# Input projections of a two-layer hybrid backbone: seven block products per pair of tiles in place of eight, weights in five column blocks

## What is computed

```
h_lat = rmsnorm(x, norm_g) * (1.0 + scale[:, None]) + shift[:, None]
h_ctx = rmsnorm(ctx, norm_g) * (1.0 + scale_c) + shift_c
s_lat = split_cols(h_lat @ w_in)
s_ctx = split_cols(h_ctx @ w_in)
...
q = jax.nn.silu(s["hg_q"]); z = s["hg_f"]
logf = jnp.logaddexp(log_lb, log_1mlb + jax.nn.log_sigmoid(z)); kk = (1.0 - lbh) * jax.nn.sigmoid(-z)
xbc = jax.nn.silu(dwconv_centred(s["ss_xbc"], conv_w, conv_b))
y = jnp.concatenate([br[0] for br in branches], axis=-1) @ w_out
```

## Time and profile before

| | us |
|---|---|
| median of three runs (5851.4 to 5854.6) | 5852.31 |
| the profiled execution's own time | 5848.45 |
| its span, first to last instruction | 5846.7 |
| layer 0's projection, first to last product | about 1136 |
| TensorE busy | 5392.3 (92% of the span) |
| VectorE busy | 2994.9 (51%) |
| ScalarE busy | 1701.4 (29%) |
| GpSimd busy | 2398.8 (41%) |
| DMA, mean over the span | 91 GB/s |

### The profile page before, as it was taken

One profiled execution on the slowest core, in us unless ns is written; L12 is line 12 of the kernel. 1 busy time (PEld: TensorE's weight loads), 2 busy tenths in 40 slices (PEclk: granted clock), 3 DMA queues, 4 the chain that ended last, 5 costly groups with the idle time before them and its releaser, 6 DMA issues. The chain is left out here.

```text
span 5846.7 us, 74555 instructions
## 1 busy us (share of the span) xinstructions
PE 5392.3 (92%) x25984; PEld 2843.0 (49%) x25984; DVE 2994.9 (51%) x5002; ACT 1701.4 (29%) x4084; POOL 2398.8 (41%) x1761
## 2 busy tenths in 40 slices
PE   5999999987888799999889999999678889999989
PEld 2445445436777533333445544544467763333334
DVE  1444444444777655551334455455557766555324
ACT  1121121122344244444112212212224432444422
POOL 0112212223444279998211112111234434999941
PEclk7999999986999899999899999999779998999999
DMA  6233233247222100000543333332462211000022
GB/s 241 86 104 101 99 100 102 96 170 238 89 91 95 57 1 8 8 1 6 214 149 109 101 99 103 101 98 95 138 200 97 95 51 46 1 8 8 5 110 106
DMA packets 358609, 530.08 MB, mean 91 GB/s; under 512 B 89344, under 2 KB 233528, under 8 KB 351904
## 3 DMA queue, kind: packets, MB, share of 16 engines
q1 hardware_dynamic: 332818, 457.34, 23.6%
q10 hardware_dynamic: 19728, 40.41, 1.8%
q0 software_dynamic: 5760, 28.36, 1.4%
HBM read 371.61 MB, written 154.08 MB: 90 GB/s over the span
## 5 line engine op out<-in xcount | busy, mean ns | idle before, releaser
L607 PE MATMUL psum<-group_W,projection_hT 128*128 128x512 f32 (+3 forms) x4304 | 1686.1, 547 | 5.9 <-DVE projection_hT L729 5.7
L2277 POOL TENSOR_TENSOR attention_PS<-attention_PS 128x1024 f32<-128x1024 f32 x548 | 1265.7, 2350 | 81.2 <-ACT attention_PS L2410 72.9
L607 PEld LDWEIGHTS psum<-group_W,projection_hT 128*128 128x128 f32 x4304 | 814.2, 190 | 841.6 <-issue 805.8
L2323 DVE TENSOR_REDUCE attention_mxp<-psum 128x1 f32<-128x512 f32 (+1 forms) x1016 | 654.5, 686 | 541.6 <-PE psum L2460 541.6
L459 POOL TENSOR_TENSOR projection_cx<-projection_cx,projection_cw 128x768 f32<-128x768 f32 x102 | 188.4, 1847 | 1684.9 <-DMA projection_cw<-in_ss_conv_w 1684.9
L2410 ACT ACTIVATE attention_PS<-psum 128x512 f32<-128x512 f32 (+1 forms) x1168 | 630.6, 591 | 717.3 <-PE psum L2514 689.4
L2460 PE MATMUL psum<-attention_QK 32*128 32x512 f32 (+1 forms) x2592 | 771.5, 611 | 9.1 <-DVE attention_mxp L2312 6.1
L2508 PE MATMUL psum<-attention_QK 32*128 32x512 f32 x2336 | 664.3, 642 | 0.0
L2526 PE MATMUL psum<-attention_PS,attention_va 128*64 128x512 f32 x2336 | 627.7, 616 | 0.0
L607 PE MATMUL psum<-projection_W,projection_hT 128*128 128x512 f32 (+3 forms) x1424 | 563.0, 538 | 8.3 <-DMA projection_W<-in_w_in 8.3
L680 ACT ACTIVATE projection_ut<-psum 128x256 f32<-128x256 f32 (+2 forms) x322 | 127.5, 407 | 1426.5 <-PE psum L607 1416.4
(11 more groups left out here) (386 smaller groups left out, 6627.1 us busy)
## 6 DMA issues: line engine op xcount, KB each, us to landing
u<-projection_ut SPq DMA_DIRECT2D x240, 256.0 KB, 2.0
projection_cx<-xbc SPq DMA_DIRECT2D x306, 128.0 KB, 2.2
projection_cw<-in_ss_conv_w SPq DMA_DIRECT2D x102, 384.0 KB, 4.5
mixing_hg<-u SPq DMA_DIRECT2D x34, 1024.0 KB, 5.0
group_W<-in_w_in SPq DMA_DIRECT2D x8, 2316.0 KB, 18.9
output_y<-y SPq DMA_DIRECT2D x34, 512.0 KB, 4.1
xbc<-projection_ut SPq DMA_DIRECT2D x34, 384.0 KB, 2.4
projection_cx<-in_ss_conv_b SPq DMA_DIRECT2D x102, 128.0 KB, 3.7
```

The source lines that it names most:

```text
L607: ins = nc.tensor.matmul(ps[n % RING][:, lo - c0:lo - c0 + w], hT[b][:, q], W[q][:, lo:lo + w], start=(q == 0), stop=(q == KT - 1))
L2277: G.tensor_tensor(SA[x % 2][:, rs, 0:w], one[:, rs, 0:w], PT[i % PTB][:, rs, 0:w], ALU.add) \
L2323: bk.release(V.tensor_reduce(mxp[x % 2][:, q:q + nn, 2 * pr + j, a], bk[job, j][:, 0:nn * (hi - lo)].rearrange("p (q n) -> p q n", q=nn), ...
```

## The change

The projection of both layers is written anew; modulation, output and the allocation of weights follow.

- The columns are sorted into five blocks (`COLUMNS`), each with a left and a right half of up to 512 columns (268 in block 3). The tiles go in nine pairs, the pairs in three groups of three. The order is group, block, pair; one pair in one block is called a **quad** here, and 3.1 is block 3, second pair of its group. 45 quads a layer.
- A quad takes seven products of 4 matmuls each (P1, P6, P7, P5, P2, P4, P3) into four banks A, B, D, E. ScalarE copies P1 out of A and P2's sum to `u`; VectorE makes yy = P6 + P1, ff = P7 + yy, C22 = P5 + ff, then P4 + yy and P3 + yy. TensorE waits for p1 ahead of P2, for ff ahead of P4 and for C22 ahead of P3; the next quad's P1 waits for A, its P7 for D and its P5 for E. In the last layer the context pair is multiplied directly ("simple").
- VectorE makes T1 and T2 of the next block in the last quad of a block; GpSimd makes T3 and T4 there, and S1 to S4 once a pair.
- Weights are held for two blocks only (`k.raw`) and loaded again in each of the three groups (57 MB a layer for 19 MB). SP issues the load when a block's first quad starts.
- What follows the product (gates, rotation, forget gate) runs one quad later, in four steps (`stage1` to `stage4`) placed between the additions. Gates are Exp on ScalarE, then +1, reciprocal and product on VectorE, as before, for both tiles at once and from SBUF instead of PSUM.
- The convolution goes in two pieces of 384 columns a tile, assigned to quads by `CONV`: one a quad from quad 1.1 on; the groups have 10, 12 and 14 pieces for 11, 11 and 10 places, so that a second piece comes into 3.0 in group 1 and into 3.0, 3.1, 3.2, 4.0 in group 2 (groups are counted from 0).
- In the output stages GpSimd no longer waits for the weights; SP loads two weight blocks of layer 1 during output0.

```diff
+COLUMNS = [([(OFF["ss_xbc"], 512)], [(OFF["ss_xbc"] + 512, 256), (OFF["ss_z"], 256)]),
+           ([(OFF["hg_f"], 512)], [(OFF["hg_q"], 256), (OFF["hg_i"], 256)]),
+           ([(OFF["da_q"], 512)], [(OFF["ml_o"], 256), (OFF["ml_z"], 256)]),
+           ([(OFF["da_z"], 256), (OFF["ml_i"], 12)], [(OFF["hg_z"], 256), (OFF["ml_i"] + 12, 4), (OFF["ss_dt"], 8)]),
+           ([(OFF["ml_v"], 256), (OFF["da_v"], 256)], [(OFF["ml_q"], 512)])]
 BANKS = 8
...
+def load_block(k, eng, l, i, some):
+
+    for n in some:
+        at = 0
+        for lo, w in COLUMNS[i % len(COLUMNS)][n % 2]:
+            rows = k.x["w_in"][l, (n // 2) * 512:(n // 2 + 1) * 512, lo:lo + w].rearrange("(k p) n -> p k n", p=P)
+            eng.dma_start(k.raw[i % 2][n][:, :, at:at + w], rows).then_inc(k.b_in[i % 2], 16)
+            at += w
...
+    TURN = {0: 1, 1: 2}
+    for g in range(GROUPS - 1):
+        TURN[quad_of[g, NB - 1, 1]] = 3 * g + 3
+        TURN[quad_of[g, NB - 1, 2]] = 3 * g + 4
+        TURN[quad_of[g + 1, 0, 0]] = 3 * g + 5
+    CONV_TILES = [range(0, 5), range(5, 11), range(11, NT)]
+    CONV = {q: [] for q in range(N)}
+    jobs = []
+    for g in range(GROUPS):
+        some = [(g, c, t) for c in range(2) for t in CONV_TILES[g]]
+        slots = [quad_of[g, b, j] for b in range(1, NB) for j in range(MEMBERS)][1:]
+        if g == GROUPS - 1:
+            slots = slots[:-1]
+        extra = [quad_of[g, b, j] for b, j in ((3, 0), (3, 1), (3, 2), (4, 0))][:max(0, len(some) - len(slots))]
+        for job, q in zip(some, sorted(slots + extra)):
+            CONV[q].append(len(jobs))
+            jobs.append(job)
...
+                def taps(m):
+                    g, c, t = jobs[m]
+                    part = slice(c * CWD, c * CWD + CWD)
...
+                    for a in range(3):
+                        sp.dma_start(cx[:, a], k.xbc[t + 1, a:a + P, part]).then_inc(s["taps_in"], 16)
...
+                for q in range(N):
+                    if first_of(q) and 1 <= inst(q) < INST - 1:
+                        sp.wait_ge(s["product"], products(q))
+                        load_block(k, sp, l, inst(q) + 1, range(4))
+                    if CONV[q]:
+                        taps(CONV[q][0])
+                    if q:
+                        store(q - 1)
+                    if len(CONV[q]) > 1:
+                        taps(CONV[q][1])
...
+                for q in range(N):
+                    if q and simple(q - 1):
+                        gp.wait_ge(s["product"], products(q))
+                        t3(inst(q))
+                    for m in CONV[q]:
+                        convolve(m)
+                    if last_of(q) and q + 1 < N:
+                        if not simple(q + 1):
+                            t3(inst(q + 1))
+                        produced(gp, q, "P4")
+                        t4(inst(q + 1))
+                    if q in TURN:
+                        sums(TURN[q])
...
-                def products(r, b, n, kind):
...
-                    for q in some:
-                        ins = nc.tensor.matmul(ps[n % RING][:, lo - c0:lo - c0 + w], hT[b][:, q], W[q][:, lo:lo + w],
-                                               start=(q == 0), stop=(q == KT - 1))
...
+                    at_least(pe, s["free_A"], made("A", q))
+                    product("A", a11, b11, w, True)
+                    at_least(pe, s["free_B"], made("B", q))
+                    pe.wait_ge(s["t12_made"], 2 * i + 2)
+                    pe.wait_ge(s["sums_made"], 4 * p + 2)
+                    product("B", S2, T2, w, True)
+                    at_least(pe, s["free_D"], made("D", q))
+                    pe.wait_ge(s["t3_made"], i + 1)
+                    pe.wait_ge(s["sums_made"], 4 * p + 3)
+                    product("D", S3, b12, w, True)
+                    at_least(pe, s["free_E"], made("E", q))
+                    product("E", S1, T1, w, True)
+                    if q in TURN:
+                        turn(TURN[q])
+                    pe.wait_ge(s["p1_made"], full(q + 1))
+                    product("A", a12, b21, w, False)
+                    pe.wait_ge(s["t4_made"], i + 1)
+                    pe.wait_ge(s["ff_made"], full(q + 1))
+                    product("D", a22, T4, w, False)
+                    pe.wait_ge(s["c22_made"], full(q + 1))
+                    pe.wait_ge(s["sums_made"], 4 * p + 4)
+                    product("E", S4, b22, w, False)
...
+                def conv_gate(m):
+                    act.wait_ge(s["conv_sum"], m + 1)
+                    A(cx[:, 1], cx[:, 0], ACT.Exp, scale=-1.0).then_inc(s["conv_sig"], 1)
...
+                    for m in CONV[q][:1]:
+                        conv_gate(m)
...
+                        produced(act, q, "P2")
+                        A(u[q % 2][:, 0, 0:w], bank["A"][:, 0:w], ACT.Copy).then_inc(s["free_A"], 1)
+                    for m in CONV[q][1:]:
+                        conv_gate(m)
...
+                        z, sig = v[:, :, 768:1024], e[:, :, 256:512]
+                        st.then(V.tensor_scalar(e[:], e[:], 1.0, None, ALU.add))
+                        V.reciprocal(v[:, :, 512:768], e[:, :, 0:256])
+                    else:
+                        z = v[:].rearrange("p t (h n) -> p t h n", h=2)[:, :, :, 0:256]
+                        sig = e[:].rearrange("p t (h n) -> p t h n", h=2)
+                    if b != 2:
+                        st.then(V.tensor_scalar(sig, sig, 1.0, None, ALU.add))
+                    st.then(V.reciprocal(sig, sig))
+                    V.tensor_tensor(z, z, sig, ALU.mult).then_inc(s["gated"], 1)
+
...
+                def stage2(q):
+                    n = of_block(1, q + 1)
+                    if block(q) == 1:
+                        z = u[q % 2][:, :, 0:512]
+                        dve.wait_ge(s["lf_log"], n)
+                        at_least(dve, s["st_kk"], 16 * (n - 1))
+                        if l:
+                            st.then(V.scalar_tensor_tensor(h1[:], z, 0.0, h1[:], ALU.min, ALU.subtract))
+                            st.then(V.tensor_tensor(h1[:], h1[:], lbr[:, 0].unsqueeze(1).to_broadcast([P, 2, 512]), ALU.add))
+                            V.tensor_tensor(h2[:], h1[:], z, ALU.subtract).then_inc(s["lf_key"], 1)
+                        else:
+                            V.scalar_tensor_tensor(h2[:], z, 0.0, h1[:], ALU.max, ALU.add).then_inc(s["lf_key"], 1)
+                            V.scalar_tensor_tensor(z, z, 0.0, h1[:], ALU.min, ALU.subtract).then_inc(s["lf_done"], 1)
+                        return
+                    if block(q) == 2:
+                        rotate(q, 1)
+                    multiply(q)
...
+                def stage3(q):
+                    n = of_block(1, q + 1)
+                    if block(q) == 1 and l:
+                        z = u[q % 2][:, :, 0:512]
+                        lb1 = lbr[:, 1].unsqueeze(1).to_broadcast([P, 2, 512])
+                        dve.wait_ge(s["lf_key"], n)
+                        st.then(V.tensor_tensor(z, h1[:], lb1, ALU.subtract))
+                        V.scalar_tensor_tensor(h0[:], z, -1.0, z, ALU.mult, ALU.min).then_inc(s["lf_neg2"], 1)
+                        st.then(V.tensor_tensor(h1[:], h1[:], lb1, ALU.max))
+                    if block(q) == 1:
+                        multiply(q)
...
+                def convolved(m):
+                    dve.wait_ge(s["conv_sig"], m + 1)
+                    st.then(V.tensor_scalar(cx[:, 1], cx[:, 1], 1.0, None, ALU.add))
+                    st.then(V.reciprocal(cx[:, 1], cx[:, 1]))
+                    at_least(dve, s["st_conv"], 16 * m)
+                    V.tensor_tensor(co[:], cx[:, 0], cx[:, 1], ALU.mult).then_inc(s["conv_done"], 1)
...
+                    if q:
+                        stage1(q - 1)
+                    if not simple(q):
+                        produced(dve, q, "P6")
+                        dve.wait_ge(s["p1_made"], full(q + 1))
+                        V.tensor_tensor(yy[:, 0:w], bank["B"][:, 0:w], p1[:, 0:w], ALU.add).then_inc(s["free_B"], 1)
+                    if q:
+                        stage2(q - 1)
+                    if not simple(q):
+                        produced(dve, q, "P7")
+                        dve.wait_ge(s["free_B"], made("B", q + 1))
+                        V.tensor_tensor(ff[:, 0:w], bank["D"][:, 0:w], yy[:, 0:w], ALU.add).then_inc(s["ff_made"], 1)
+                    if q:
+                        stage3(q - 1)
+                    if not simple(q):
+                        produced(dve, q, "P5")
+                        dve.wait_ge(s["ff_made"], full(q + 1))
+                        at_least(dve, s[f"st_u{q % 2}"], stored(q - 2))
+                        V.tensor_tensor(v[:, 1, 512:512 + w], bank["E"][:, 0:w], ff[:, 0:w], ALU.add).then_inc(s["c22_made"], 1)
+                    if last_of(q) and q + 1 < N:
+                        t12(inst(q) + 1, 1)
+                        t12(inst(q) + 1, 2)
+                    if q in TURN:
```

(16 more changed lines are left out.)

786 lines of the change are left out of this document (384 added, 402 removed).

## The result

The changed kernel takes **5950.54 us** in the median (5943.75 to 5956.28) against 5853.45 (5851.4 to 5857.88) for the kernel before: a ratio of 1.0164, 95% interval 1.0147 to 1.0182. Forecast were 5871 us and a range up to 5940. The sign, slower, had the larger chance; the size was missed: the profiled execution, 5950.89 us, lies 102.4 us above that of before, where the sum gave 19. The result lies in the band of the prediction's "port or further waits" (5900 to 6030), which had a chance of 0.25.

What follows compares the result with a forecast made beforehand. TensorE, busy 92% of the span, was taken to bound the kernel, chiefly by projection matmuls. From 5848 us, 303 saved and 322 given back made 5867; with 3.9 for the median, 5871 us, range 5790 to 5940.

Steps and rivals of the forecast that it cites:

- port or further waits: Outcome band of 5900 to 6030 us, for the shared SBUF port deciding or more waits; chance 0.25.
- What takes time away: Both projections: seven products for eight save 141.5 us in layer 0 and 126 in layer 1, together 267.
- The starts and tails: Projections' beginnings and ends: gains of 9 us at layer 0's start, 3 at layer 1's, 8 for both tails.
- the outputs: Both output stages: GpSimd's sums no longer wait for weights, so the second product starts earlier; 16 us saved.
- the sum of the stalls: Waits added in the projections: 135 us in layer 0 and 187 in layer 1, 322 in all.
- Stalls in front of ff: TensorE's sixth product waits behind VectorE's gates: 1.75 us each in 2.1 and 2.2, 6.2 in 3.1 and 3.2.
- the queue: At block starts, taps land behind weights at about 16 us: 3.0 loses 9.75 us, 2.0 loses 2, per group.
- the rule that I had weighed: SP's DMA queue: each engine consumes descriptors in ring order; had taps overtaken weights, 3.0 would be about 1 us shorter.
- The step that failed: Layer 1's forget gate: VectorE operations meeting GpSimd end after it, 1.86 instead of 0.69 us; whole term 52 us.
- The rival of 6016 us: SBUF port: GpSimd lengthens VectorE's two-tensor operations by 1.17 us, 200 us in all; band 5900 to 6030, chance 0.25.
- Doubled quads: Quads with a second convolution piece, a 14 us chain: 12.5 us lost in group 1, 34 in group 2.
- new convolution weights: Convolution chains of groups 1 and 2: newly loaded weights add 3 us each, within 52 us a layer.

Runs made afterwards that it cites:

- e3: Changed kernel with SP issuing the convolution piece's store and taps and the previous quad's stores ahead of the next block's weight load: 5962.0 us.
- e2: Changed kernel with T3 and T4 of the weights made by VectorE in place of GpSimd: 5929.8 us.
- e4: Changed kernel with the convolution pieces spread over more quads, double places only in 4.0 and 4.1 of group 2: 5845.3 us.
- e7: Changed kernel with ScalarE's copy of P2 (in context quads, their copies) ahead of the convolution piece's Exp: 5948.7 us.
- e1: Changed kernel with the gates' sigmoids on ScalarE (Exp, Ln, Exp) in place of VectorE's +1 and reciprocal: 5852.7 us.
- e8: Kernel before with only the output change: GpSimd makes the first pair's sums ahead of its weight wait and next-layer loads: 5841.2 us.

## Why the prediction missed

**What takes time away** was right. By the undisturbed quads (24.03 and 12.66 us) it is 142.5 us in layer 0, forecast 141.5, and 129 in layer 1, forecast 126. A product step is 0.858 us where I had 0.865, a narrow one 0.452 where I had 0.473. The starts and tails gave 28 us, forecast 20; the outputs 12.6, forecast 16. What failed is the sum of the stalls: 322 us forecast; with the narrow step as measured, 179 us in layer 0 and 234 in layer 1.

**Stalls in front of ff** were sized rightly in the quads computed: 2.2 and the narrow ones with one piece are within 1 us of the forecast lengths, 3.0 in groups 1 and 2 too (in group 0, where it waits for new convolution weights as well, it is 2.4 us longer). In layer 1, where GpSimd's T3 and T4 were counted, 2.0 of groups 1 and 2 lost 13.6 and 13.4 us for 13.2. e3 bears out the queue as well: issued ahead of the weights, the taps of 3.0 landed early and the quad of group 0 took 21.5 us for 25.4. By that the rule that I had weighed (the Trainium skill, DMA: Bandwidth & Descriptors, Queues, rings and completion order) agrees with the runs.

**The step that failed** is the one on GpSimd beside VectorE. I counted it for the forget gate of layer 1 alone and gave the rival a flat 1.17 us on half of all operations. What the trace shows is neither: a few operations are held until a long one of GpSimd ends (0.35 us becomes 4.67), at each turn of a block, and quads behind it pay. In layer 0, 2.0, 2.1 and 4.0 lost 51.5 us where I had 24.3. e2 shows what of the whole gap is T3 and T4: 21 us of run time, net of the 4.6 us a turn that VectorE took on. For 4.0 of group 0 I had written no loss at all and it was 6.5 us (3.2 in e4, where VectorE came first). T1, T2 and a piece in the last quad before it, 4.6 + 3.7 us, should have been added to that quad's list just as the gates were. How 4.0's 26.6 us divide between this list, GpSimd's convolution beside it and the second piece, no run separates fully: without T3 and T4 on GpSimd it was still 22.7, with the pieces spread (e4) 10.2. The Trainium skill (SBUF — State Buffer, SBUF: two separate sides) calls the shared ports an exclusive lock, held for the whole instruction by whichever engine starts first. The traces agree: the operation of 4.67 us ended within 0.3 us of T3's end, and in e2, without a T3 on GpSimd, the same line's mean is 354 ns. The rival of 6016 us named this mechanism; its price was too high: e2 took 80 us of held-up time away and gained 21.

**The step that was missing** is the context quad of layer 1. I took its products out of the gain but left its chain (a piece, 14 us and more) out of the losses: TensorE stood 14.2 and 15.2 us there, and layer 1's first group lost 67.5 us for 48. The trace shows the waits, but no run shows the chain to be the whole cause: with ScalarE's copies ahead of the piece (e7) the group was only 2 us shorter, since the same piece stands ahead of bank D's addition on VectorE.

**Doubled quads** were right in kind and short in layer 0 by 17 us, or by 11 if the 6 us put down for new convolution weights are counted to them: 3.1 of group 1 took 38.2 us for 32, with TensorE waiting 11.7 us for p1 and 8.9 for ff. That e4's gain of 106 us matches the forecast 104 is partly luck: these quads lost more than forecast, and e4's new places cost something of their own (13.3 us in 3.0 of group 2 for 9.1).

The range was made from the sizes of stalls that were in the sum; quads that I had set to zero (4.0 with one piece, layer 1's context quads) were not among its cases.

## What to carry to other kernels

Where an engine works a list in order, add up that list for every kind of step, the short ones most: the average (VectorE at 61% in layer 0) said nothing, and the steps with least TensorE work lost most. Taking the wait that is seen away buys only the distance to the next one: e1 removed 135 us of waits for ff and gained 98 us, e7 removed 34 us of waits for copies and gained 2, and moving T3 and T4 off GpSimd was worth 21 us with VectorE late and 3 without (single executions each). A change that loses can hold a win: with the follow-up work moved to the engine that was 28% busy, the pieces spread and the lists reordered, the seven products gave 4% over the kernel before. No run gave the kernel before the same gates on ScalarE; in its layer-0 projection TensorE stands nowhere (1135.5 us busy in 1135.5 from first to last product), so little is to be expected of it.

## What the runs showed of the hardware

VectorE's operations with two SBUF operands, and its scalar additions from SBUF to SBUF, end only after the GpSimd operation under way (4.67 us for 0.35 beside a T3 of 6.61). In the projections of the changed kernel 81 such operations began under a GpSimd operation that would outlast them, and all 81 ended behind it, by nearly their own length: 0.22 us for one of 0.35, 0.55 for 0.69, 1.08 for 1.22. Its reciprocal from SBUF (72 times 2553 ns, 14 of them under such an operation) and its operations with one operand in PSUM (91 of them) were never held. It works the other way as well: T3 took 6.61 us where VectorE's T2 (2.29) was under way first, and 4.50 where it wasn't. On the clock: behind a wait of 6.52 us eight narrow half-instructions took 3.80 us for 1.97, behind 2.85 us eight wide ones 5.37 for 3.60 (granted clock 0.68), but behind 3.60 us of wait in e8's output only 3.70 (granted clock 1.00). Within the changed kernel's projections eight wide ones took 5.40 us behind a wait of 2.30 in one place (granted clock 0.69) and 3.70 behind 2.31 in another (1.00). The length of the wait alone did not tell the loss.
